# Fifty-six throw-away products on TensorE in four attention-head hand-overs and one output block of a hybrid attention step

## The chip, the cores and the metric

The program runs on one core of one Trainium2 chip, in one launch. The metric is the device time of that launch in microseconds (us), and several executions of the kernel are summarised by their median. The engines are named as in the profile: PE is TensorE, PEld its weight loads, DVE is VectorE, ACT is ScalarE, POOL is GpSimd, SP is the engine that issues most of the transfers.

## The reference

The reference is one layer of a streaming encoder on 512 prompt frames and 64 new frames, 1024 features wide:

```
h   = x + 1/2 * SwiGLU_1(RMSNorm(x))                 # d_ff 2816
u   = RMSNorm(h);  proj = u @ w_in                   # q, k, v of two groups of heads, rotary on q and k
oa  = sliding-window attention with sinks            # group A: 8 query heads, 2 key/value heads, 64 wide
ob  = softmax(q1 k1) v - lam * softmax(q2 k2) v      # group B: 4 heads, 128-wide values, block-causal
ob  = RMSNorm per head and frame (ob) * g_subln * (1 - lam_init)
h   = h + concat(oa, ob) @ w_out
h   = h + 1/2 * SwiGLU_2(RMSNorm(h));  y = RMSNorm(h)
```

It returns y for prompt and new frames, and the new key and value caches.

## The kernel before

All activations lie transposed, features on the partitions and the 576 frames along the free axis, so that one product of a weight block of 128 x 128 covers 288 frames and two of them cover all. For accuracy each weight block and each activation is split into a high part (made by ACT, `w_hi`, L950) and a low part (made by DVE, `w_lo`, L1291), and each product is done three times: high by high, high by low, low by high. These are the products of line L594 (`feature_products`); one step `k` of a block is six of them. The two feed-forward parts take the first 450 us and the last 400 us or so; between them lie projections, attention and the output projection.

The middle part is one list of events, written once by `make_schedule` and walked by every engine, each taking from an event what is its own:

- `k (b, k)`: step k of the projection of q/k tile b, and, for b = 13, of output block 0. They are the filling between the attention steps.
- `S n`: the scores of unit n on PE (L799 for prompt tiles of group B, L803 for the new frames), the row maxima on DVE (L1604 to L1616), the exponentials on ACT (L1184, L1188).
- `N n`: normalising the probabilities on DVE (L1628 to L1639).
- `T r`: transposing them on PE (L828, into PSUM bank `T_BANK`) and copying them to SBUF on ACT (`probs_t`, L1209).
- `O r`: the product with the values on PE (L864, L868), and, after a head's last tile, copying the output out on DVE (`o_b`, L1666, L1668) and squaring it on ACT (L1224).
- `R`: once per B head, the per-head RMSNorm: sum of squares on DVE (L1675), square root on ACT (L1230, with a table load before it), reciprocal and five scalings of `o_b` on DVE (L1682, L1684), which raise `ob_ready`.
- `L`: once per B head, `heads_back`: PE waits for `ob_ready` and transposes the normalised output back (L881 four times, L882 once); ACT writes `mix_hi` (L1238, L1239) and DVE `mix_lo` (L1692, L1695), which raise `mix_ready`.

Each engine works through its own instructions strictly in the order of the list. For heads 0, 1 and 2 the order on all engines around the hand-over is `O` of the next head's first tile, `L`, `T` and `N`, then `S` of the next head's last tile. That last `S` waits on PE for the exponentials of the tile before it, whose PSUM banks it reuses. Of output block 0 (b = 13) the steps 0 to 6 stand between the attention events of heads 2 and 3; its step 7 needs the mix of head 3 and is the last event of all. The end of the list is:

```
T[39](B,3,3)   O[39](B,3,3)   R(head 3)   L(head 3)   k(13,7)
```

After it PE goes through output blocks 1 to 7, eight steps each, in `out_step`. Block 0 waits, at each of its steps, for the part of the mix that this step reads (`if d == 0: pe.wait_ge(mix_ready, ...)`); block 1 waits at its step 0 for the last exponentials and the last mix, since it writes into PSUM banks that attention used. Block d from 2 on waits for the addition of block d - 2 to the residual.

At the start of the program PE does 44 products of a 128 x 128 tile of ones with itself in fp32 (L733, `WARM_UP`), until the first inputs are there. Each product shows as two matmul records in the trace.

Of the kernel before, what the change touches and what calls it, by code (L numbers as in the profile page):

```python
# [25 lines left out]
P = 128  # L26
# [12 lines left out]
B_HEADS = 4  # L39
# [65 lines left out]
def split_base(key):  # L105

    kind = key[0]
    if kind == "qk" and key[1] == len(TILES) - 1:
        return SPLIT_Z
    return (SPLIT_X, SPLIT_Y)[key[-1] % 2]  # L110
# [38 lines left out]


WARM_UP = 44

Y_GP = 2

# [94 lines left out]
def hybrid_step(nc, a, o):  # L249

    stack = ExitStack()
    with stack:
        def sb(name, shape, dt=FP32, where=stack):
            return where.enter_context(nc.sbuf_tensor(name, shape, dt))
# [12 lines left out]
        ones = sb("ones", [P, P])  # L267
# [52 lines left out]
        acc = stack.enter_context(nc.psum_tensor("acc", [P, 8, BANK], FP32))  # L320
# [79 lines left out]
        T_BANK, O_BANK = 6, 7  # L400
# [76 lines left out]
        def mix_tile(n):  # L477
            return UNITS[n][1] + (PAIRS if UNITS[n][0] == "L" else 0)

        def pair(n):  # L480

            return 2 + 2 * (order_at[n] % 2)

        def wait_scores_banks(pe, n):

            if order_at[n] < 2:
                return
            former = bank_order[order_at[n] - 2]
            if UNITS[former][0] == "L":
                pe.wait_ge(mix_ready, mix_count[former])  # L490
            else:
                pe.wait_ge(exp_done, score_at[former] + 1)
# [91 lines left out]
        def _(pe):  # L584
            def block_ready(key):

                pe.wait_ge(split_ready, GROUP[key] + 1)

            def feature_products(bank, base, k_in_block, hi, lo, k, first, last, token_halves=(0, 1)):

                col = base + k_in_block * P
                for n, (w_part, x_part) in enumerate(((w_hi, hi), (w_hi, lo), (w_lo, hi))):
                    for t in token_halves:
                        m = nc.tensor.matmul(acc[:, bank + t, 0:HALF], w_part[:, col:col + P],  # L594
                                             x_part[:, k, t * HALF:(t + 1) * HALF],
                                             start=first and n == 0, stop=last and n == 2)
                return m
# [133 lines left out]

            for _ in range(WARM_UP):
                nc.tensor.matmul(acc[:, NORM_BANK, 0:P], ones[:], ones[:], start=True, stop=True)  # L733
# [3 lines left out]
            for c in range(2):  # L737
                for kc in range(2):
                    key = ("v", 2 * c + kc)
                    block_ready(key)  # L740
                    for tt in range(TOK_TILES):
# [8 lines left out]
                        for k in range(V_K):  # L750
# [4 lines left out]
                            for n, (x_part, w_part) in enumerate(((u_hi, w_hi), (u_hi, w_lo), (u_lo, w_hi))):  # L755
# [3 lines left out]
                                    start=kg == 0 and n == 0, stop=kg == KD - 1 and n == 2)  # L759
# [77 lines left out]
            def values(r):  # L837
# [33 lines left out]
                                         v_new[0:DEC, SEQ_TILES, P * (t + 1):P * (t + 2)], start=False, stop=True)  # L871
                m.then_inc(o_done, 1)

            def heads_back(n):
                h = UNITS[n][1]
                wait_scores_banks(pe, n)

                pe.wait_ge(ob_ready, h + 1)
                bank = pair(n)
                for tt in range(SEQ_TILES):  # L880
                    nc.tensor.transpose(acc[:, bank, tt * P:(tt + 1) * P], o_b[:, h % 2, tt, :], ident[:])  # L881
                nc.tensor.transpose(acc[:, bank + 1, 0:DEC], o_b[0:DEC, h % 2, SEQ_TILES, :],  # L882
                                    ident[0:DEC, 0:DEC]).then_inc(ob_turned, 1)

            def out_step(d, k):

                bank = 2 * (d % 2)
                if k == 0:
                    block_ready(("out", d))
                    if d >= 2:  # L890

                        pe.wait_ge(res_ready, KD + d - 1)
                    elif d == 0:
                        pe.wait_ge(x_out, len(TILES))
                    else:

                        pe.wait_ge(exp_done, len(score_order))
                        pe.wait_ge(mix_ready, mix_count[bank_order[-1]])
                if d == 0:

                    pe.wait_ge(mix_ready, max(c for n, c in mix_count.items() if mix_tile(n) == k))
                m = feature_products(bank, split_base(("out", d)), k, mix_hi, mix_lo, k, k == 0, k == KD - 1)
                if k == KD - 1:
                    m.then_inc(block_used, 1)

            for event in EVENTS:
                if event[0] == "k":
                    _, b, k = event
                    if b == len(TILES):
                        out_step(0, k)  # L910
                        continue
                    if k == 0:
                        block_ready(("qk", b))
                        if b == 0:

                            pe.wait_ge(v_out, TOK_TILES + 2)
                        elif b == 1:

                            pe.wait_ge(v_out, 2 * TOK_TILES)
                        else:  # L920

                            pe.wait_ge(x_out, 1 if b == 2 else b)
                    m = feature_products(tile_bank(b), split_base(("qk", b)), k, u_hi, u_lo, k, k == 0, k == KD - 1)
                    if k == KD - 1:
                        m.then_inc(block_used, 1)
                elif event[0] == "S":
                    scores(event[1])
                elif event[0] == "T":
                    transposes(event[1])
                elif event[0] == "O":  # L930
                    values(event[1])
                elif event[0] == "L":
                    heads_back(event[1])

            for d in range(1, KD):
                for k in range(KD):
                    out_step(d, k)
# [1002 lines left out]
```

## Time and profile before

| | |
|---|---|
| median of 3 runs | 1163.64 us (1162.18 to 1164.63) |
| the profiled execution | 1164.48 us |
| its span, first to last instruction | 1162.7 us |
| PE busy | 1093.1 us, 94% of the span |
| DVE busy | 702.2 us, 60% |
| ACT busy | 477.0 us, 41% |
| POOL busy | 88.7 us, 8% |
| mean granted TensorE clock | 0.968 of full |

The 1.8 us between the span and the execution's own time lie outside the first and the last instruction. In the profile a granted clock of 1.00 is TensorE's full rate of 2.4 GHz and 0.50 is 1.2 GHz. The busy time of a matmul counts from its start to the end of its way through the array, so consecutive matmuls overlap in it; the rate is read from the starts. A profile row gives in brackets the idle time of the engine just before that row and what ended it.

### The profile page before, as it was taken

Reading aid. Unit: us, or ns where it says so; the run is one execution under the profiler, and the core shown is the slowest. Engines: PE = TensorE matmul, PEld = TensorE weight load, DVE = VectorE, ACT = ScalarE, POOL = GpSimd, SP = SyncE. Lnnn points to the kernel's source line nnn. Section 1 sums busy time; section 2 is a strip of 40 time slices with the busy share of each in tenths; the row PEclk is TensorE's granted clock in tenths of the full one; section 3 lists DMA queues with packets and bytes.
Section 4 is the critical chain, followed back from the end, with each engine's and each line's share of the span. In section 5 each row is a group of like instructions: output and inputs, shape, how many; then the busy total and the mean of one; then the engine's idle time right before and its main releaser. Section 6 shows DMA issues by size and latency. Waiting matters only on the chain.

```text
span 1162.7 us, 18955 instructions
## 1 busy us (share of the span) xinstructions
PE 1093.1 (94%) x7874; PEld 1057.8 (91%) x7874; DVE 702.2 (60%) x1046; ACT 477.0 (41%) x803; POOL 88.7 (8%) x84
## 2 busy tenths in 40 slices
PE   9989999999999999778898859999999999999995
PEld 9989999999999999766777639999999999999994
DVE  5887832588863333556677744478883248886324
ACT  6445531256553333223344443334563125555221
POOL 0000000000001111312222102200000000000012
PEclk9999999999999999888999869999999999999997
DMA  5233123222222241300021102223313222222202
GB/s 191 74 109 109 54 97 103 93 81 102 98 76 76 94 140 60 123 19 27 21 73 37 50 1 73 79 84 111 110 50 101 91 105 76 107 96 76 77 26 82
DMA packets 22660, 94.43 MB, mean 81 GB/s; under 512 B 2928, under 2 KB 6000, under 8 KB 18096
## 3 DMA queue, kind: packets, MB, share of 16 engines
q1 hardware_dynamic: 22576, 93.23, 24.0%
q8 instruction: 63, 1.03, 0.4%
q14 instruction: 21, 0.17, 0.0%
HBM read 88.24 MB, written 4.98 MB: 80 GB/s over the span
## 4 chain that ended last, share of the span: by engine, by line
PE 75%; DVE 14%; ACT 6%; issue 4%; POOL 0%; DVEq 0%; ACTq 0%; POOLq 0%
PE acc L594 34%; PE acc L663 33%; PE acc L756 3%; ACT w_hi L950 2%; DVE w_lo L1291 1%; PE acc L733 1%; ACT c_hi L1028 1%; DVE comb L1405 1%; PE acc L851 1%; DVE st L1605 1%; DVE st L1598 1%; ACT probs L1174 1%; ACT probs L1184 1%; DVE probs L1639 1%; DVE res L1740 1%
## 5 line engine op out<-in xcount | busy, mean ns | idle before, releaser
L1291 DVE TENSOR_TENSOR w_lo<-raw,w_hi 128x1024 fp32r<-128x1024 f32 (+3 forms) x145 | 175.5, 1211 | 266.8 <-ACT w_hi L950 266.0
L663 PE MATMUL acc<-c_hi,w_hi 128*128 128x288 f32 x952 | 282.5, 297 | 5.5 <-DVE w_lo L1291 5.5
L663 PE MATMUL acc<-c_lo,w_hi 128*128 128x288 f32 x952 | 283.3, 298 | 0.0
L663 PE MATMUL acc<-c_hi,w_lo 128*128 128x288 f32 x952 | 283.3, 298 | 0.0
L950 ACT ACTIVATE w_hi<-raw 128x1024 fp32r<-128x1024 f32 (+3 forms) x145 | 149.1, 1028 | 190.6 <-PE acc L594 175.3
L594 PE MATMUL acc<-h_hi,w_hi 128*128 128x288 f32 x1024 | 222.7, 297 | 3.9 <-DVE w_lo L1291 3.9
L594 PE MATMUL acc<-h_lo,w_hi 128*128 128x288 f32 x1024 | 221.6, 296 | 0.0
L594 PE MATMUL acc<-h_hi,w_lo 128*128 128x288 f32 x1024 | 221.5, 296 | 0.0
L663 PEld LDWEIGHTS acc<-c_hi,w_hi 128*128 128x128 f32 x952 | 179.9, 189 | 6.0 <-DVE w_lo L1291 6.0
L663 PEld LDWEIGHTS acc<-c_lo,w_hi 128*128 128x128 f32 x952 | 179.8, 189 | 0.0
L663 PEld LDWEIGHTS acc<-c_hi,w_lo 128*128 128x128 f32 x952 | 179.5, 189 | 0.0
L594 PEld LDWEIGHTS acc<-h_hi,w_hi 128*128 128x128 f32 x1024 | 166.0, 188 | 4.8 <-DVE w_lo L1291 4.6
L594 PEld LDWEIGHTS acc<-h_lo,w_hi 128*128 128x128 f32 x1024 | 165.9, 188 | 0.1
L594 PEld LDWEIGHTS acc<-h_hi,w_lo 128*128 128x128 f32 x1024 | 165.9, 188 | 0.0
L1291 DVE TENSOR_TENSOR w_lo<-comb,w_hi 128x1024 fp32r<-128x1024 f32 x68 | 83.3, 1225 | 60.7 <-ACT w_hi L966 60.7
L966 ACT ACTIVATE w_hi<-comb 128x1024 fp32r<-128x1024 f32 x68 | 71.8, 1056 | 68.3 <-PE acc L663 37.6
L1056 ACT ACTIVATE comb<-acc 128x288 f32<-128x288 f32 x136 | 56.1, 412 | 103.2 <-PE acc L663 103.0
L1768 POOL TENSOR_TENSOR ssq<-ssq,sq 128x576 f32<-128x576 f32 x23 | 33.7, 1465 | 848.0 <-issue 720.1
L594 PE MATMUL acc<-u_hi,w_hi 128*128 128x288 f32 x208 | 54.0, 343 | 1.5 <-DVE sq L1579 1.4
L594 PE MATMUL acc<-u_lo,w_hi 128*128 128x288 f32 x208 | 47.4, 312 | 0.0
L594 PE MATMUL acc<-u_hi,w_lo 128*128 128x288 f32 x208 | 47.3, 311 | 0.0
L594 PEld LDWEIGHTS acc<-u_hi,w_hi 128*128 128x128 f32 x208 | 35.8, 205 | 12.3 <-issue 11.8
(198 smaller groups left out, 1327.6 us busy)
## 6 DMA issues: line engine op xcount, KB each, us to landing
raw<-in_w1gu SPq DMA_DIRECT2D x17, 1024.0 KB, 4.8
raw<-in_w2gu SPq DMA_DIRECT2D x17, 1024.0 KB, 4.8
raw<-in_w1d SPq DMA_DIRECT2D x16, 704.0 KB, 4.1
raw<-in_w2d SPq DMA_DIRECT2D x16, 704.0 KB, 4.1
raw<-in_w_qk SPq DMA_DIRECT2D x13, 512.0 KB, 3.6
raw<-in_w1gu SPq DMA_DIRECT2D x10, 512.0 KB, 4.6
raw<-in_w2gu SPq DMA_DIRECT2D x10, 512.0 KB, 3.7
raw<-in_w_out SPq DMA_DIRECT2D x8, 512.0 KB, 3.5
```

Of the source, the lines that this page charges most:

```text
L594: m = nc.tensor.matmul(acc[:, bank + t, 0:HALF], w_part[:, col:col + P], x_part[:, k, t * HALF:(t + 1) * HALF], start=first and n == 0, st ...
L663: m = nc.tensor.matmul(acc[:, banks[side(f)], 0:HALF], w_part[:, col:col + P], x_part[:, k, c, :], start=n in (P1, P5, P2) and k == 0 and ...
L733: nc.tensor.matmul(acc[:, NORM_BANK, 0:P], ones[:], ones[:], start=True, stop=True)
L756: m = nc.tensor.matmul(acc[0:n_tok, V_BANK[tt], 0:V_HALF], x_part[:, kg, tok], w_part[:, split_base(key) + k * V_HALF:split_base(key) + (k ...
L851: m = nc.tensor.matmul(acc[rows, O_BANK, tile * P:(tile + 1) * P], v_new[:, tile - 1 + s, HEAD * part:HEAD * part + HEAD], pt[:, (2 * qi + ...
L950: nc.scalar.activation(cols, src, ACT.Copy).then_inc(hi_ready, 1)
L966: nc.scalar.activation(w_hi[:, first * PART:(first + 2) * PART].rearrange("p (s n) -> p s n", s=2), w_sum[:, 2 * half:2 * half + 2, :], AC ...
L1028: nc.scalar.activation(c_hi[:, j, 1:PARTS, :], b[:, 2:PARTS + 1, :], ACT.Copy).then_inc(chi_ready, 1)
L1056: nc.scalar.activation(to, acc[:, PRODUCTS[n][0][side(f)], 0:HALF], ACT.Copy).then_inc(snapped, 1)
L1174: m = nc.scalar.activation(pr[:, 256 * s:256 * (s + 1)], acc[:, bank + s // 2, 256 * (s % 2):256 * (s % 2 + 1)], ACT.Exp, scale=SCALE, bia ...
L1291: return nc.vector.tensor_tensor(cols, src, hi.bitcast(FP32), ALU.subtract).then_inc(split_ready, 1)
L1768: nc.gpsimd.tensor_tensor(ssq[:], ssq[:], sq[:], ALU.add).then_inc(ssq_added, 1)
```

## The change

`keep_going(n)` is added on PE: n fp32 products of the 128 x 128 tile of ones with itself, written into the first 128 columns of `T_BANK`, which nobody reads. It is called in `heads_back` between the wait for the PSUM banks and the wait for `ob_ready`, with 9 products for heads 0 to 2 and 20 for head 3, and in `out_step` at step 0 of output block 1, between the wait for the block's weights and the waits for the last exponentials and the last mix, with 9 products. In all that is 3 x 9 + 20 + 9 = 56 products. Nothing is removed or moved.

```
+KEEP, KEEP_LAST = 9, 20
...
+            def keep_going(n):
+                for _ in range(n):
+                    nc.tensor.matmul(acc[:, T_BANK, 0:P], ones[:], ones[:], start=True, stop=True)
+
             def heads_back(n):
                 h = UNITS[n][1]
                 wait_scores_banks(pe, n)
+                keep_going(KEEP_LAST if h == B_HEADS - 1 else KEEP)
 
                 pe.wait_ge(ob_ready, h + 1)
...
                     elif d == 0:
                         pe.wait_ge(x_out, len(TILES))
                     else:
 
+                        keep_going(KEEP)
                         pe.wait_ge(exp_done, len(score_order))
                         pe.wait_ge(mix_ready, mix_count[bank_order[-1]])
```

## Rows read from the trace of the kernel before

**Rows 1.** The page: PE's busy tenths and granted clock by slices; the final chain by engine.

```profile
PE   9989999999999999778898859999999999999995
...
PEclk9999999999999999888999869999999999999997
...
PE 75%; DVE 14%; ACT 6%; issue 4%; POOL 0%; DVEq 0%; ACTq 0%; POOLq 0%
```

**Rows 2.** Waits of PE, 480 to 700 us: total, times, longest.

```profile
PE acc L881 <- DVE o_b L1684: 6.7, 4, 4.5
PE acc L799 <- ACT probs L1184: 6.6, 3, 2.3
```

**Rows 3.** Timeline of PE at head 0, and one wait before it.

```profile
603.42 1.16 PE L864 MATMUL acc<-v_new,probs_t 128*128 128x128 f32 x8 [1.13 <-ACT probs_t L1209]
...
616.51 0.63 PE L881 MATMUL acc<-ident,o_b 128*128 128x128 f32 x4 [0.65 <-DVE o_b L1684]
...
617.47 0.44 PE L828 MATMUL acc<-ident,probs 128*128 128x128 f32 x2
620.21 1.22 PE L799 MATMUL acc<-k_b,q_b 64*128 64x512 f32 x4 [2.30 <-ACT probs L1184]
...
631.68 0.60 PE L828 MATMUL acc<-ident,probs 128*128 128x128 f32 x4
```

**Rows 4.** Windows: length, PE busy, granted clock, DMA share, GB/s.

```profile
602.00:604.00 2.00, 0.87 (x9) 1.00 0.00 0
621.20:624.40 3.20, 3.20 (x14) 0.50 0.00 0
648.50:655.10 6.60, 4.98 (x16) 0.50 0.10 37
679.30:682.40 3.10, 1.46 (x11) 1.00 0.00 0
682.60:686.00 3.40, 2.64 (x11) 0.50 0.00 0
694.40:699.60 5.20, 5.20 (x22) 0.50 0.02 3
700.00:747.00 47.00, 47.00 (x355) 1.00 0.26 84
```

**Rows 5.** Timelines of PE at heads 2 and 3.

```profile
671.36 0.63 PE L881 MATMUL acc<-ident,o_b 128*128 128x128 f32 x4 [0.77 <-DVE o_b L1684]
...
675.05 2.08 PE L799 MATMUL acc<-k_b,q_b 64*128 64x512 f32 x4 [2.05 <-ACT probs L1184]
...
684.48 2.07 PE L864 MATMUL acc<-v_new,probs_t 128*128 128x128 f32 x8 [0.69 <-ACT probs_t L1209]
...
691.03 1.09 PE L881 MATMUL acc<-ident,o_b 128*128 128x128 f32 x4 [4.48 <-DVE o_b L1684]
692.05 0.37 PE L882 MATMUL acc<-ident,o_b 64*128 64x64 f32 x1
694.37 0.85 PE L594 MATMUL acc<-mix_hi,w_hi 128*128 128x288 f32 x2 [1.96 <-DVE mix_lo L1695]
```

**Rows 6.** The warm-up: its timeline row, then windows as in rows 4.

```profile
1.08 12.77 PE L733 MATMUL acc<-ones 128*128 128x128 f32 x88 [1.08 <-DVE eps L1347]
...
3.00:5.00 2.00, 2.00 (x11) 1.00 0.93 339
7.50:9.50 2.00, 2.00 (x20) 1.00 1.05 429
```

**Rows 7.** Timelines of ACT and DVE after heads 0 and 1.

```profile
619.96 0.69 ACT L1238 ACTIVATE mix_hi<-acc,lam 128x512 fp32r<-128x512 f32 x1
...
631.89 0.01 DVE L1577 LOAD_MASK_SELECT ssq<-acc  x1 [0.81 <-PE acc L594]
...
661.89 0.16 DVE L1628 RECIPROCAL st<-st 128x1 f32<-128x1 f32 x1 [0.90 <-ACT probs L1188]
```

**Rows 8.** The final chain after head 2 and at head 3.

```profile
682.68 1.13 PE acc L828 x4
...
689.81 1.08 DVE o_b L1684 x5
...
694.37 48.20 PE acc L594 x342
```

More of the change, by code:

```diff
@@ L151 @@
 WARM_UP = 44
+KEEP, KEEP_LAST = 9, 20
 Y_GP = 2
@@ L872, in values, with keep_going @@
                 m.then_inc(o_done, 1)
+            def keep_going(n):
+                for _ in range(n):
+                    nc.tensor.matmul(acc[:, T_BANK, 0:P], ones[:], ones[:], start=True, stop=True)
             def heads_back(n):
@@ L876, in heads_back @@
                 wait_scores_banks(pe, n)
+                keep_going(KEEP_LAST if h == B_HEADS - 1 else KEEP)
                 pe.wait_ge(ob_ready, h + 1)
@@ L895, in out_step @@
                     else:
+                        keep_going(KEEP)
                         pe.wait_ge(exp_done, len(score_order))
```

## The prediction

> **What bounds the kernel now.** I read the page first: PE is near full for most of the run and carries 75% of the chain that ended last, but in the middle, slices 16 to 23, its busy share and its granted clock dip together [rows 1]. The change lives there. The list of PE's waits says what it stood for: the normalised output of the four B heads (`ob_ready`), 6.7 us in four waits with the longest of 4.5, and the exponentials before a head's last scores, 6.6 us in three waits of up to 2.3 [rows 2]. The timeline of one hand-over shows their order: at head 0 PE waits 0.65 us at L881, transposes, waits 2.30 us at L799, and then runs without a gap to 631.68 [rows 3]. Head 1 repeats it. The windows give the second price of such waits: right after the pair of waits at head 0 the clock is at 0.50 (1.2 GHz) from about 621.2 to 624.4, after head 1 from 648.5 to 655.1, and at head 3 from 682.6 to 699.6 but for nothing in between [rows 4]. The work runs at half rate there: from 694.4 to 699.6 some 21 matmuls start in 5.2 us, 0.24 us each, against 353 in 47.0 us at full clock, 0.133 us each (the counts less one or two already under way) [rows 4].
>
> So a throw-away product can do three things: nothing (the wait was longer and the clock stays as it was), cost its own time (where PE would have worked), or buy clock for the real work behind it.
>
> **What a product costs.** The warm-up is the same operation on the same operands. Its 88 records start over 12.5 us [rows 6]. At full clock 20 records are seen in 2.0 us, some two of them already under way, so 0.111 us for one; early on, at half rate, 11 in 2.0 us, less one or two, 0.2 to 0.223; I take twice 0.111, 0.223 [rows 6]. (The granted clock is printed as 1.00 there, since the trace has no record of it before its first change; the rate of the records tells the level.) A product is two records: 0.22 us at full clock, 0.45 at half. Nine are 2.0 us (4.0 at half), twenty 4.45 us (8.9 at half).
>
> **Heads 0 to 2, nine products each.** The products start where PE came free, some 0.7 us before its L881 row [rows 3, 5], take 2.0 us, and so push L881 back by about 1.3 us. What is queued behind them on PE is the transposes L881 and L882 and the next tile's L828, 1.3 us of work, then the scores at L799. Who waits for L881: ACT's `mix_hi`, which at head 0 starts only at 619.96, behind the exponentials; the transposes end at about 617.4 now and would end at 618.7. L828's copy on ACT comes behind `mix_hi`. So both are covered by ACT's exponentials, with about 1.2 us left, and the scores themselves wait for the exponentials until 620.21 as before. Direct cost: nothing. If that cover were gone it would be 1.3 us a head.
>
> What they may buy is the clock. The 2.30 us wait shrinks to about 1.0, and the first wait vanishes. The trace has a wait of 1.13 us at 603.42 behind which the clock stayed at 1.00 [rows 3, 4]; behind 0.65 and 2.30 it fell. The rest is nearer to the first, so I take it that the clock holds after heads 0 and 1 more often than not. What is that worth? At head 0, 3.4 us at half rate hold up work by about 1.5 to 1.9 us, all of it ahead of L828 at 631.68. But DVE, which takes the projection tile from PE at 631.89, had then stood idle for only 0.81 us [rows 7]: before that it was busy with the next tile's maxima and could not have taken it sooner. So of 1.9 us only 0.8 arrives: -0.8 us. After head 1 the same stretch ends in DVE waiting for ACT at 661.89, not for PE [rows 7]; ACT's exponentials there follow DVE's maxima, which follow the split of the next weights, none of it waiting for PE. There I take 0. Head 2: behind it the final chain stays on DVE and ACT until the transposes at 682.68 [rows 8], so whatever the clock does from 672 to 679 changes nothing; and then PE is too short of work to keep the clock: 0 again. Sum for the three heads: -0.8, with bounds of 0 (clock falls anyway) and -0.8 for head 0, and some -0.4 more for head 1 at best.
>
> One rule of the Trainium skill speaks against the holding. "TensorE: Matmul & The Clock Gate", section "A second HAM failure mode: psum-queue depth-cycling", says that short idles between groups of matmuls, often repeated, can make the clock swing too. The trace agrees in that waits of 0.65 and 2.30 us with work between were enough, though the 1.13 us wait was not. By that rule the -0.8 would be 0; it is one of the rivals below.
>
> **Head 3, twenty products.** Here ACT and DVE are on the path from the values at 684.48 to `ob_ready` at about 690.9, and PE is free from about 686.5 [rows 5, 8]. The clock is at 0.50 when the products begin: it fell at 682.6, and from 686 to 691 nothing here can have raised it but the products themselves [rows 4]. All at half rate they end at 686.5 + 8.9 = 695.4; all at full rate at 691.0. How soon does a run of them raise the clock? The warm-up shows the rate doubled between the windows 3 to 5 and 7.5 to 9.5, having started at 1.08 [rows 6]; head 0's stretch shows a return 3 to 4 us after dense work began at 620.21 [rows 3, 4]. With the same here, the values at 684.48 already being dense, I put the return at about 689.4. Until then 2.9 / 0.223 = 13 records, and the other 27 take 27 x 0.111 = 3.0 us: end at 692.4. That is 1.4 us later than L881's 691.03. In return L881 and L882 run at full clock: at head 0 they take 0.96 us from the first to the next instruction, here 1.39 to the end, so about 0.5 us is won. Net +0.9 us on the path, since ACT's `mix_hi` and DVE's `mix_lo` follow at once and PE waits for both [rows 5]. Bounds: the return at 688 gives +0.1 (end at 691.7), the return 5.6 us after 686.5 as late as in the warm-up gives an end of 693.8 and +2.2, and no return at all +4.4.
>
> **Output block 1, nine products.** The name of the change speaks of a wait there. There is none: PE resumes at 694.37 with step 7 of block 0, the 1.96 us wait before it is for DVE's `mix_lo` of head 3 [rows 5], and from there the final chain is one piece of PE work of 342 products in 48.2 us [rows 8]. The two waits behind the call were already met by step 7 of block 0, which needs the same mix. So the nine products lie fully on the path: 18 x 0.111 = +2.0 us. At half clock they take 4.0, but then they also use up half-rate time in which real work would have stood, so the net is again 2.0. Nothing later gives it back, since block after block follows PE, and the sums and the second feed-forward part follow those. Bounds: 1.9 to 2.4.
>
> **The clock when PE resumes.** Before, PE ran 5.2 us at half rate after 694.4 [rows 4], which cost 5.2 x (1 - 0.133 / 0.24) = 2.3 us. Afterwards the products leave PE at full clock when head 3's transposes are done; then comes the untouched wait of 1.96 us. It is nearer to the 2.05 to 2.30 us waits behind which the clock fell [rows 3, 5] than to 1.13. So I take it to fall, but from full clock, with the half-rate stretch as long as head 0's 3.4 us rather than 5.2: 3.4 x 0.446 = 1.5 us lost, that is -0.8. Bounds: 0 (as long as before), -2.3 (never falls).
>
> **Sum.** -0.8 + 0.9 + 2.0 - 0.8 = +1.3 us, against the profiled execution's 1164.48. The median of the runs shown is 0.84 lower, 1163.64, so the forecast is 1164.9 us. A measurement of this kernel can tell about 0.2%, 2.3 us, from no change.
>
> **The rivals.**
> - The clock holds over the last wait too. For it: PE is dense before and behind it. Against: the length. Then -2.3 in place of -0.8: -0.2, 1163.4 us. Still no change that can be told.
> - The skill's short idles: nothing is held after head 0 either. +2.1, 1165.7 us.
> - Faster: the clock holds through head 2's end to the values of head 3, so L828 and L864 run at full rate: 0.5 + 0.9 us, from 1.13 to 0.6 and from 2.07 to 1.16 [rows 3, 5, 8]. The twenty then begin at 685.1 at full clock, end with `ob_ready`, and cost nothing; the gain of 0.5 at L881 stays, and the last wait holds. -0.8 - 1.4 - 0.5 + 2.0 - 2.3 = -3.0, 1160.6 us. Against it: from 679.3 to 682.4 PE starts only 11 matmuls at full clock and then falls [rows 4], and no product is put there.
> - Slower: the twenty overrun. It decides from a return of the clock later than about 691.4, which puts their end at 693.4: then +1.9 at head 3, +2.0 at the output block, -0.8 at resuming and 0 or -0.8 at head 0, +2.3 to +3.1. With the warm-up's 5.6 us it is +2.2 + 2.0 + 0 + 0 = +4.2, 1167.8 us; with no return at all +6.4, 1170.0 us.
> - The change does nothing, every product hidden: 1163.6. Against it stands the missing wait at the output block.
>
> **How the numbers follow.** Forecast 0.48, clock held over the last wait 0.19, nothing held 0.10, all these within 0.2% of before; faster 0.07; slower 0.16, of which most near +3. A few hundredths of the forecast's own spread pass each bound, since three runs of the same kernel already lie 2.4 us apart: faster 0.08, same 0.73, slower 0.19. The range leaves out the faster case and half of the slower one: 1161.9 to 1167.2.
>
> **What would show it.** L881 at head 0 near 617.8 and L799 still near 620.2, with 1.00 in the windows from 621 to 624; the last 0.8 us earlier at DVE's L1577. At head 3, forty records of the new line from 686.5 (less what head 0 won) to about 692.4, with 0.50 turning to 1.00 near 689.4, and L881 directly behind them with no idle. Eighteen records between step 7 of block 0 and block 1, with no idle next to them. The forecast is wrong if L881 of head 3 still waits for `ob_ready` (then the twenty are hidden and the sum falls by 0.9 or more), if the clock at resuming stays at 1.00 or stays at 0.50 for 5 us, or if PE had idle time ahead of block 1.

## The result, and the profile after

The changed kernel takes 1165.1 us (median of 19 executions, 1163.5 to 1169.89) against 1163.62 us before (19 executions, 1161.8 to 1164.82). The ratio is 1.0020, 95% interval 1.0011 to 1.0028, that is +2.3 us, from +1.3 to +3.3. The forecast was +1.3 us, 1164.9 us. So the total came out near the forecast, but, as the experiments show, partly for another reason.

The profiled execution of the changed kernel is the slowest of the 19 (1169.89 us, span 1168.1 us). 2.7 us of its distance to the profile of before lie ahead of the first product added for the heads: the tile of scores that DVE starts to reduce at 573.68 us before is started at 576.37 us here. From there on the two can be compared stage by stage.

The timeline of PE in the changed kernel, with the added products on L880, the transposes of the heads on L890 and L891, the scores on L801, values on L866 (rows 3 and 5 of before answer to it):

```profile
618.37 2.17 PE L880 MATMUL acc<-ones 128*128 128x128 f32 x18
620.38 0.60 PE L890 MATMUL acc<-ident,o_b 128*128 128x128 f32 x4
620.91 0.28 PE L891 MATMUL acc<-ident,o_b 64*128 64x64 f32 x1
621.12 0.44 PE L830 MATMUL acc<-ident,probs 128*128 128x128 f32 x2
622.87 1.13 PE L801 MATMUL acc<-k_b,q_b 64*128 64x512 f32 x4 [1.32 <-ACT probs L1194]
...
662.03 0.66 PE L830 MATMUL acc<-ident,probs 128*128 128x128 f32 x4 [1.39 <-DVE probs L1649]
662.62 0.49 PE L801 MATMUL acc<-k_b,q_b 64*128 64x128 f32 x4
664.24 1.59 PE L866 MATMUL acc<-v_new,probs_t 128*128 128x128 f32 x8 [1.13 <-ACT probs_t L1219]
665.62 2.21 PE L835 MATMUL acc<-diag,probs 128*128 128x64 f32 x10
...
674.78 0.59 PE L866 MATMUL acc<-v_new,probs_t 128*128 128x128 f32 x2 [2.10 <-ACT probs_t L1219]
675.17 3.74 PE L880 MATMUL acc<-ones 128*128 128x128 f32 x18
678.75 0.60 PE L890 MATMUL acc<-ident,o_b 128*128 128x128 f32 x4
...
690.67 5.31 PE L880 MATMUL acc<-ones 128*128 128x128 f32 x40
695.83 0.60 PE L890 MATMUL acc<-ident,o_b 128*128 128x128 f32 x4
...
698.59 0.59 PE L596 MATMUL acc<-mix_hi,w_hi 128*128 128x288 f32 x2 [1.96 <-DVE mix_lo L1705]
...
699.94 3.32 PE L880 MATMUL acc<-ones 128*128 128x128 f32 x18
703.02 0.51 PE L596 MATMUL acc<-mix_hi,w_hi 128*128 128x288 f32 x2
```

At head 0 the products fill the first wait and push back the transposes, and the scores still wait, now 1.32 us instead of 2.30 [rows 3]. At head 3 the forty records run straight into the transposes with no idle between. In output block 1 the eighteen records stand between real products with no idle on either side. New against before are the 1.39 us wait at 662.03 and what follows it. Before, PE had no wait at the same transposes (L828) and a shorter one at the values behind them:

```profile
660.83 0.60 PE L828 MATMUL acc<-ident,probs 128*128 128x128 f32 x4
...
662.39 1.16 PE L864 MATMUL acc<-v_new,probs_t 128*128 128x128 f32 x8 [0.55 <-ACT probs_t L1209]
```

The windows of the changed kernel's profile (length, PE busy, granted clock, DMA share, GB/s) say what the clock did:

```profile
623.00:650.00 27.00, 25.88 (x187) 1.00 0.07 20
665.00:671.50 6.50, 6.50 (x29) 0.50 0.00 0
675.10:678.30 3.20, 3.20 (x17) 0.50 0.01 3
688.90:692.00 3.10, 3.10 (x15) 0.50 0.00 0
699.00:702.20 3.20, 3.20 (x16) 0.50 0.00 0
703.50:750.00 46.50, 46.50 (x351) 1.00 0.25 80
```

The half-rate stretches after heads 0 and 1 [rows 4] are gone. In their place there is one from 665 to 671.5, where PE was at full clock before. And the chain that ended last shows that this one counts:

```profile
664.24 1.59 PE acc L866 x8
665.83 2.01 PE acc L835 x10
667.84 1.16 PE acc L801 x4
668.99 1.90 PE acc L870 x8
670.89 0.63 PE acc L872 x2
...
674.78 0.59 PE acc L866 x2
675.37 3.54 PE acc L880 x18
678.91 0.44 PE acc L890 x4
...
690.88 5.11 PE acc L880 x40
```

Head 2's nine products, mostly at half rate, are themselves on the chain for 3.54 us, and head 3's twenty for 5.11 us.

To compare kernels in spite of what happened to the clock earlier in each execution, I split each profile at the starts of five DVE instructions that all the kernels have: the reduction of the new frames' scores of head 0 (L1607, 573.68 us before), the taking of projection tile 11 behind head 0 (631.89, the L1577 of [rows 7]), the copy of head 3's output (L1668, 686.59), head 3's first `mix_lo` (L1692, 693.38), and the split of weights that follows output block 1 (L1291, 705.35). The stages, in us, are differences of these starts; "last" runs to the end of the span, and "mix to block 1" holds PE's resuming and output block 1:

| profile of | to tile 11 (head 0) | to head 3's output (heads 1, 2) | to mix_lo (head 3) | mix to block 1 | last |
|---|---|---|---|---|---|
| before | 58.21 | 54.70 | 6.79 | 11.97 | 457.35 |
| changed | 57.32 | 57.23 | 6.67 | 13.26 | 457.25 |
| e1 heads only | 57.34 | 57.28 | 6.64 | 11.16 | 460.24 |
| e2 block only | 58.21 | 54.72 | 6.79 | 14.03 | 458.75 |
| e3 head 3 only | 59.55 | 54.31 | 7.92 | 9.66 | 458.85 |
| e4 heads 0 to 2 only | 57.35 | 57.35 | 6.79 | 11.17 | 460.07 |
| e5 feed-forward waits only | 58.20 | 54.75 | 6.79 | 11.91 | 457.34 |
| e6 nearly all waits | 57.34 | 53.62 | 6.17 | 9.65 | 456.91 |
| e7 heads and mix wait | 57.34 | 54.82 | 7.19 | 9.65 | 458.81 |
| e8 block twice | 59.52 | 54.35 | 6.79 | 16.55 | 460.29 |
| e9 heads 0 to 2, later waits | 57.34 | 56.24 | 6.78 | 11.63 | 457.30 |
| e10 heads 0 to 2, feed-forward | 57.34 | 57.38 | 6.79 | 11.20 | 457.29 |
| e11 placed by wait | 57.35 | 53.68 | 6.18 | 9.66 | 457.40 |
| e12 twelve at head 3, mix wait | 58.19 | 54.81 | 6.18 | 9.65 | 460.32 |

Each profile is one execution; the medians and ratios below are over 5 to 12 executions of each kernel, with 27 to 35 of before beside them.

### The profile page after: what moved, and what is told of

It reads as the page before. It is cut to its first block, busy times and chain, and to the rows that moved or that the text cites. A ratio compares the mean times of both kernels' runs of the same rounds, so it can differ in the third digit from the quotient of the medians.

```text
span 1168.1 us, 19175 instructions
## 1 busy us (share of the span) xinstructions
PE 1105.5 (95%) x7986; PEld 1072.1 (92%) x7986; DVE 702.0 (60%) x1046; ACT 476.7 (41%) x803; POOL 88.6 (8%) x84
## 4 chain that ended last, share of the span: by engine, by line
PE 75%; DVE 15%; ACT 6%; issue 3%; POOL 0%; DVEq 0%; ACTq 0%; POOLq 0%
PE acc L596 34%; PE acc L665 33%; PE acc L758 3%; ACT w_hi L960 2%; DVE w_lo L1301 2%; PE acc L735 1%; PE acc L880 1%; PE acc L853 1%; DVE st L1615 1%; ACT c_hi L1038 1%; DVE comb L1415 1%; ACT probs L1194 1%; DVE probs L1649 1%; DVE st L1608 1%; ACT probs L1184 1%
```

## The experiments

**The change taken apart.** Four kernels were measured together: the four heads without the block, the block without the heads, head 3 alone, and heads 0 to 2 alone.

```
e1: KEEP_AT, KEEP_OUT = (9, 9, 9, 20), 0     e2: (0, 0, 0, 0), 9
e3: (0, 0, 0, 20), 0                         e4: (9, 9, 9, 0), 0
+                keep_going(KEEP_AT[h])      # heads_back
+                        keep_going(KEEP_OUT)   # out_step, block 1
```

> The change without the nine products of output block 1 (heads 9, 9, 9, 20 stay). Theory 1, the nine lie bare on PE's path: 2.0 us below the changed kernel, about 1163.1 us and the ratio to before near 1.000 (0.9985 to 1.0005). Theory 2, the nine are hidden or pay for themselves in clock, and the loss comes from the heads: no faster than the changed kernel, 1165.1 us, ratio 1.0013 or more.

Measured: 1161.07 us (1159.31 to 1168.47), ratio 0.9994, interval 0.9978 to 1.0010. By the medians it is 4.0 us below the changed kernel, which was timed on another occasion; by the ratios, each against runs of before of its own occasion, it is 0.26%, 3.0 us. That is at least the 2.0 us of theory 1; theory 2 does not fit. The 12 executions are far apart: eight between 1159.3 and 1162.4 us with a mean granted clock of 0.977 to 0.981, four between 1165.8 and 1168.5 us with 0.973.

> Only the nine products of output block 1, none in the heads. Theory 1: before plus 2.0 us, 1165.6 us, ratio 1.0017. Theory 2: as before, ratio 1.000. In the profile 18 records of the new line with no idle on either side by theory 1; idle shortened by as much by theory 2.

Measured: 1164.76 us (1162.78 to 1168.58), ratio 1.0019, interval 1.0006 to 1.0033. That is theory 1, and its profile shows it without detour:

```profile
691.92 0.85 PE L596 MATMUL acc<-mix_hi,w_hi 128*128 128x288 f32 x2 [1.96 <-DVE mix_lo L1705]
...
693.52 3.84 PE L880 MATMUL acc<-ones 128*128 128x128 f32 x18
697.12 0.51 PE L596 MATMUL acc<-mix_hi,w_hi 128*128 128x288 f32 x2
```

No idle on either side; and the stage from the mix to block 1 is 14.03 us against 11.97, +2.06 us. The records ran mostly at half rate, 3.6 us from the first to the next real product, and the net is 2.06 all the same. PE is at half rate for 5.1 us after it resumes here (691.92 to 697.0) and for 5.2 us before (694.37 to 699.6), so the real work that the products displaced ran at full rate behind them.

> Only the twenty products of head 3. Forecast's step: they begin at half clock, overrun ob_ready by about 1.4 us and win 0.5 us in the transposes and 0.8 us or more after PE resumes: between +0.1 and -0.9 us, ratio 0.9992 to 1.0001. If the twenty end by ob_ready: -1.3 us or better, ratio 0.9985 to 0.999. If their overrun outweighs the clock: +1 us or more, ratio 1.001.

Measured: 1161.94 us (1159.88 to 1164.61), ratio 0.9993, interval 0.9984 to 1.0002, inside what the forecast's step gave. In the profile the products cost and won more than forecast: they pushed head 3's `mix_lo` from 6.79 to 7.92 us (+1.13), and afterwards the clock held while PE waited for the mix, so that the next stage took 9.66 us instead of 11.97 (-2.31):

```profile
686.02 6.56 PE L880 MATMUL acc<-ones 128*128 128x128 f32 x40
692.42 0.60 PE L890 MATMUL acc<-ident,o_b 128*128 128x128 f32 x4
692.95 0.27 PE L891 MATMUL acc<-ident,o_b 64*128 64x64 f32 x1
695.19 0.54 PE L596 MATMUL acc<-mix_hi,w_hi 128*128 128x288 f32 x2 [1.97 <-DVE mix_lo L1705]
```

The clock held over the wait of 1.97 us with no product in it, as in the forecast's rival of the last wait.

> Only the nine products of each of heads 0, 1 and 2. Forecast's step: -0.8 us from head 0 and nothing from the others, ratio 0.9993. The rival, read from the profile of the changed kernel, is that the clock that they hold up is only taken away later, between the values of heads 1 to 3, where PE's work is on the path: a half-rate stretch near 665 us in its profile costs 2.4 us, so that the sum is between +0.5 and +1.5 us, ratio 1.0005 to 1.0013, in the executions that have it, and -0.8 in the others: more spread than before.

Measured: 1166.85 us (1163.31 to 1168.18), ratio 1.0027, interval 1.0017 to 1.0038. This is the surprise: the three heads' products, forecast at -0.8 us, lose 3.1 us. Its profile is the best pair to that of before, since until 566 us the clock changes at the same places within 0.3 us. By the table it wins 0.86 us at head 0, loses 2.65 between heads 1 and 3, wins 0.8 when PE resumes, and loses 2.72 in the last stage, where the two kernels have not one instruction that differs. The windows at the three places:

```profile
662.00:668.70 6.70, 6.70 (x30) 0.50 0.00 0
...
768.00:771.00 3.00, 3.00 (x14) 0.50 0.49 168
815.60:818.90 3.30, 2.87 (x12) 0.50 0.00 0
```

The chain of e4 carries the same two things as that of the changed kernel: values and transposes at half rate from 661.5 us, and head 2's products:

```profile
661.49 1.69 PE acc L866 x8
663.17 2.01 PE acc L835 x10
...
672.90 3.35 PE acc L880 x18
```

The last stage shows one wait twice. This is the timeline row of before, then that of e4:

```profile
766.08 0.54 PE L594 MATMUL acc<-h_hi,w_hi 128*128 128x288 f32 x2 [1.76 <-DVE w_lo L1291]
```

```profile
766.94 0.53 PE L596 MATMUL acc<-h_hi,w_hi 128*128 128x288 f32 x2 [1.76 <-DVE w_lo L1301]
```

The wait is 1.76 us in both, PE was full ahead of it in both, and in before the clock stayed at 1.00, also over the 2.54 us wait at 811 to 814 us:

```profile
764.00:767.00 3.00, 1.24 (x10) 1.00 0.01 1
811.00:814.50 3.50, 0.96 (x8) 1.00 0.00 0
814.50:818.00 3.50, 3.50 (x28) 1.00 0.32 42
```

In e4 it fell behind both. So the length of a wait does not settle whether it costs clock. The program here is the same in both kernels and the wait comes 0.86 us later in e4, so I take it that the moment at which it comes counts too; no run tests this by itself. The changed kernel's own profile happens to have none of these falls in its last stage (457.25 us).

**Is it the waits of the feed-forward parts?** The next four kernels were measured together. The products of the first two are written into the PSUM bank that the following work overwrites, or into `T_BANK` where nothing in it is still to be read, and the wait for the data comes behind them. For this some waits of PE were put into another order, and every kernel but e8 from here on has that order, also at the waits where it has no products; no kernel measures the new order by itself. In their profiles the stages without new products are within 0.11 us of those in the old order (57.34 us in e7 and in e1; 58.19 and 54.81 in e12, 58.21 and 54.70 before).

```
e5: FILL = {gate/up (0,2,up): 8, pair (0,5): 11, gate/up (1,1,up): 7, pair (1,5): 9}
+                keep_in(FILL.get(("gu", ffn, f, part), 0), acc[:, bank, 0:P])
                 block_ready(key)
```

> No products in the heads or in output block 1; instead 8, 11, 7 and 9 products in the four waits of the feed-forward parts (near 47, 81, 764 and 811 us). Theory A, raised by the runs so far: what these kernels differ in is largely whether the clock falls behind those waits, which hangs on where they come and not on their length alone. Then no half-rate stretch is left near 48, 85, 768 and 816 us, the median is 1.5 us below before (1161.2 us, ratio 0.9985 to 0.999) and the slow end of the spread (1167 us) is gone. Theory B, the spread has another origin: the spread stays and the ratio is 1.000 or above, by the products' own time.

Measured: 1163.15 us (1160.07 to 1164.15), ratio 0.9988, interval 0.9978 to 0.9998. The slowest of the 12 took 1164.15 us. Of the 27 of before on this occasion one took 1166.64 us and the others at most 1165.05, which is too little to say that a slow end is gone. The profile of e5 has no half-rate stretch in either feed-forward part up to the last wait of the run, and the last stage is 457.34 us. Theory A held in the profile and in the ratio; the median fell by 0.6 us and not by 1.5, and what it says of the spread stays open.

> Products in nearly every wait of PE over 1 us, none in output block 1: those of the feed-forward parts, 9, 9, 9 and 18 in the heads, 7 ahead of the wait for head 3's mix, and 79 in nine waits of the attention part. Theory A: nearly all half-rate stretches go, the mean clock is above 0.985, and where PE is on the path behind them it shows: 6 to 12 us below before, ratio 0.990 to 0.995. Theory B: the products cost about what they win, ratio 0.998 to 1.002.

There were in fact 93 products in ten waits of the attention part. Measured: 1160.91 us (1159.84 to 1164.66), ratio 0.9978, interval 0.9967 to 0.9989. The mean clock rose to 0.990 and the gain was 2.6 us, not 6 to 12. One reason stands in its timeline, at the longest wait of PE:

```profile
506.54 7.37 PE L596 MATMUL acc<-ones 128*128 128x128 f32 x44 [4.53 <-ACT probs_t L1241]
```

Ahead of the products PE waited 4.53 us for a copy by ACT, so the clock was already low when they began, and only some 1.4 us were left of the 5.9 us wait that they were to fill. They took 7.37 us: DVE's last `mix_lo` ahead of this place was done at 507.8 us, and the values behind it started at 513.83. Such products ahead of 575 us cost 3.2 us in all (its new frames' scores of head 0 are reduced from 575.51 us, those of e5 from 572.31); behind them every stage of e6 is the shortest or nearly so, 5.3 us below before in all.

```
e7: the change, with block 1's nine products out and
+                    if k == KD - 1:   # step 7 of block 0, ahead of the wait for head 3's mix
+                        keep_in(7, acc[:, T_BANK, 0:P])
```

> The change with the nine products of output block 1 taken out and 7 put where PE does wait, ahead of the mix of head 3 (step 7 of block 0). By the forecast's arithmetic the clock then holds when PE resumes: 1.5 us below the kernel with the heads' products alone, 3.5 us below the changed kernel: median near 1160 to 1161 us, ratio 0.9975 to 0.9985, and no half-rate stretch near 697 to 700 us. If the clock falls there all the same: as with the heads' products alone, 0.9994.

Measured: 1162.36 us (1159.54 to 1164.32), ratio 0.9989, interval 0.9978 to 1.0001. In the profile PE resumes at full clock and the stage is 9.65 us, against 11.16 with the heads alone and 13.26 in the changed kernel. That step is as forecast; the median came out 1.4 us above the top of what was expected, and its 12 executions lie in two groups, four up to 1160.4 us and eight from 1162.1 us. Here the clock fell at 647.7 us instead of 662, behind the 1.34 us that are left of head 1's wait for the exponentials, and PE then came later to the work of 657 to 664 us. That costs nothing: 54.82 us from head 0 to head 3's output, as before. Head 2's nine products ran at full rate and are not on the chain. In the changed kernel the same wait at head 1 is 1.33 us long and the clock held over it.

> Only output block 1, with 18 products in place of 9, none in the heads. If a product there costs its own 0.222 us and nothing else: +4.0 us, ratio 1.0034, twice that of nine. By theory A the total is +4.0 us give or take the stretches behind the waits near 765 and 812 us, which come later against the clock's changes: the lower group of its runs at +4 - 1.5 or +4, an upper one 2 to 4 us above.

Measured: 1168.88 us (1166.09 to 1171.96), ratio 1.0047, interval 1.0029 to 1.0066. The stage of block 1 grew by 4.58 us in the profile, 2.2 times the 2.06 of nine; 18 x 0.222 = 4.0 us of it are the products' own time at full clock. Of the rest, 0.5 us, the profile shows a longer stretch at half rate: 6.1 us after PE resumed, against 5.2 before. The last stage was 460.29 us.

**What becomes of the three heads' products.** The last four were again measured together.

```
e9:  KEEP_AT (9, 9, 9, 0), e5's FILL, and {O[33]: 5, T[34]: 5, O[34]: 4}
e10: KEEP_AT (9, 9, 9, 0), e5's FILL
e11: KEEP_AT (9, 9, 9, 18), e9's FILL, {O[24]: 4, O[36]: 8, O[38]: 10, O[39]: 3}, mix: 7
e12: KEEP_AT (0, 0, 0, 12), mix: 7
```

> The nine products of heads 0, 1 and 2 (none at head 3, none in block 1), with 14 more in the three waits of the stretch from 657 to 662 us behind head 1's hand-over, and 35 in the waits of the feed-forward parts. Theory C: the three heads' products lose because the clock that they held is then taken away behind those later waits, where PE's values and transposes are on the path, and head 2's products, run at half rate, come on the path too. Then with those waits filled the half-rate stretch near 662 to 669 us is gone in most executions, the stretch from head 0's tile hand-over to head 3's values is back from 57.3 to 54.7 us or less, and the median is 2 us or more below before, ratio 0.998. Rival: the three heads' products cost time of their own: the stretch stays at 57.3 us.

> As the run above but without the 14 products of 657 to 662 us: the nine of heads 0 to 2 and the 35 of the feed-forward parts. Theory A: the last 457 us (after output block 1) come back from 460.0 us to 457.3 us, since the clock no longer falls behind the waits near 765 and 812 us; the loss of 2.6 us between heads 1 and 3 stays: ratio near 1.0005, against 1.0027 with the heads' products alone. Rival, the loss of the heads' products lies wholly in the attention part: ratio 1.002 or more.

Measured: e10 1163.40 us (1161.5 to 1165.7), ratio 1.0002, interval 0.9993 to 1.0011; e9 1163.13 us (1161.8 to 1164.62), ratio 1.0002, interval 0.9994 to 1.0011. In e10 the last stage is back at 457.29 us and 0.25% of e4's 0.27% is gone, although the stretch between heads 1 and 3 is as long as in e4 (57.38 us). Not all of the 0.25% was e4's loss, though: the same 35 products won 0.12% without any in the heads (e5), and they also fill the two waits ahead of 100 us. The remaining 0.13%, about half of e4's 0.27%, is what the three heads' products cost at the feed-forward waits, which they don't touch; each of these differences is uncertain by some 0.1%. Against e5, e10 is still 0.14% slower. Theory A's number (1.0005) held.

Theory C of e9 held only in part. The 14 products kept the clock over the waits at 657 to 662 us, but then it fell at 667 us, in the next wait, and head 2's nine products ran at half rate and on the chain again:

```profile
667.94 0.77 PE acc L886 x2
668.71 3.84 PE acc L900 x18
```

The stage is 56.24 us, between 54.70 and 57.38, and the median gains nothing over e10.

> Only head 3: 12 products instead of 20 there, and 7 ahead of its mix. With 20, L881 came 0.5 to 1.1 us late and directly behind the products in two profiles. With 12 they end well before ob_ready even at half rate (686.5 + 5.3 = 691.8 at worst): the stretch from head 3's values copied out to its mix_lo is 6.3 to 6.8 us, against 6.8 before and 7.9 with 20 alone, and PE resumes at full clock, 6.3 us for block 1's stretch against 7.9. Together -2.3 us, ratio 0.998. If 12 are too few to hold or raise the clock: 4.09 and 7.9 us as before, ratio 1.000.

Measured: 1163.08 us (1158.13 to 1165.16), ratio 0.9992, interval 0.9979 to 1.0005. In the profile both stages came out as expected, 6.18 and 9.65 us, together 2.9 us below before; the last stage gave 3.0 us back, with half rate behind both feed-forward waits:

```profile
765.20:768.20 3.00, 3.00 (x14) 0.50 0.44 152
813.00:816.00 3.00, 3.00 (x13) 0.50 0.01 3
```

The ratio lies between the two that were expected (0.998 and 1.000). The best execution took 1158.13 us; it was not profiled, so that it had none of these falls is a guess.

> What the runs point to: 9, 9, 9 and 18 products in the heads, 7 ahead of head 3's mix, none in block 1, 25 in the waits on copied probabilities of the last tiles, the 14 of 657 to 662 us and the 35 of the feed-forward parts; none in the waits before 600 us, where the kernel with products in nearly all waits lost 3.6 us. From its stretches: -1.9 us before 92 us, -0.9 at head 0, -1.0 to head 3, -0.6 in head 3, -2.3 when PE resumes, -0.4 after: 1157 us, ratio 0.9945, at least 0.3% below the changed and the old kernel.

Measured: 1158.20 us (1156.09 to 1159.18, 5 executions), ratio 0.9956, interval 0.9944 to 0.9968: 5.1 us faster than before by the ratio, close to what was expected (0.9945), and the fastest of all. Every stage behind 574 us is at or near its shortest. From 615 to 675 us and from 679 to 1146 us its clock is at 1.00, with one fall between:

```profile
615.00:675.00 60.00, 54.43 (x394) 1.00 0.12 34
675.40:678.60 3.20, 3.00 (x13) 0.50 0.00 0
679.00:1146.00 467.00, 460.24 (x3446) 1.00 0.24 79
```

## Why the prediction was right, and where it was right by luck

**The price of a product** held: 18 records of head 0 take 2.0 us from their start at 618.37 to the transposes at 620.38, 0.112 us each; 0.111 was forecast.

**Head 0, -0.8 us**: the stage measured 58.21 before and 57.32 to 57.35 in every profile that has the products there, -0.87. The forecast had limited the gain by DVE's 0.81 us of idle time at its L1577 rather than by what PE lost at half rate, and for this profile that was the right limit. It is not the limit in every execution: the stage took 59.55 us in e3 and 59.52 in e8, which have no products there either. In these two the clock stayed low for 6.8 us behind the same waits and not for 3.4; against them the products win 2.2 us.

**Heads 1 and 2, 0 us**: this step failed, and in place of nothing there were two losses. First, the products' own time was held to be covered, worked out at full rate, and at head 2 the clock was to change nothing, "whatever the clock does from 672 to 679". At full rate, 2.0 us, they are covered (e7); mostly at half rate the nine take 3.5 us and are on the chain. Second, the forecast asked where the work behind a kept clock would gain and not where PE would then stand idle next. PE reached 657 to 664 us early, waited 1.39 and 1.13 us for DVE and ACT, and the clock fell there, ahead of values and transposes that are on the chain. Together +2.5 us in the profile (54.70 to 57.23), in e4 +2.65. By e9, whose nine are slow but whose values ahead of them are not, some 1.5 us of this belong to the first loss; that is an estimate, since e9 has 14 more products. Where the clock fell elsewhere, as in e7, the loss was 0.1 us. And the stage had something to give: with the next waits filled too, e6 and e11 took 53.62 and 53.68 us.

**Head 3, +0.9 us**: the mechanism is right, the size too large for the changed kernel. The products ran directly into the transposes, and the stage took 6.67 us instead of 6.79, because the clock rose 1.5 us after they began and not 2.9. The transposes started 0.6 us after `o_b` was scaled, where the forecast had them 1.4 us late. In e7 it rose after 2.5 us and the stage was 7.19, +0.40; in e3 after 4.1 us, 7.92, +1.13. So the term hangs on when the clock rises, as the forecast said. Twelve products do it in 6.18 us (e12).

**Output block 1, +2.0 us**: +2.10 (13.26 against 11.16 in e1), +2.06 (e2 against before). PE had no wait there, as the forecast read from the order of the list.

**Resuming, -0.8 us**: e1 against before is 11.16 to 11.97, -0.81, and in the changed kernel the clock fell from full behind the wait, for 3.4 us, as forecast. But that the size came out is luck. e4 and e10, with no product at head 3 and the clock already low through the wait, have 11.17 and 11.20 us: PE resumed in e4 at 696.06 and was back at full clock at 699.5, 3.4 us too. So these profiles do not show that head 3's products earned the 0.8 us. With 7 products ahead of this wait the clock held (e7, e12: 9.65), and in e3 it held without them (9.66), so that they are needed is not shown either.

**What the sum left out**: the waits near 765 and 812 us. One fall behind them costs about 1.45 us (457.35 to 458.8), two 2.9 (460.2). The profile of before has neither; the other kernels shift by up to a few microseconds what comes at them, and their profiles have one, both or none. This, with heads 1 and 2, is a loss the forecast did not have. Against it stands only the smaller cost at head 3. That the total nevertheless stayed near +1.3 is no merit of the forecast: the median rose by 1.5 us, the ratio says +2.3, and the changed kernel's profile has no late fall while e4's has two. The stage table adds up for the profiled pair: -0.89 + 2.53 - 0.12 + 1.29 - 0.10 = +2.7 us, and another 2.7 us of that profile lie ahead of the change.

Of the rivals, nothing held after head 0 did not happen, though short waits did cost clock elsewhere. The Trainium skill, "TensorE: Matmul & The Clock Gate", section "A second HAM failure mode: psum-queue depth-cycling", says that short idles between groups of matmuls, when they come often enough, make the clock swing. The runs agree in so far as waits of 1.40 and 1.13 us with work between them did it at 662 us in e4. They do not agree for head 0 of the changed kernel, where a single 1.32 us wait was left and the clock held. The other rival, the clock held over the last wait, came true in e3 and not in the changed kernel.

What stays open: what sets the moments at which a wait costs clock. Kernels with the same instructions from 700 us on take the late falls in one profile and not in another, so the order of the instructions there does not settle it. And why e4's executions take the late falls so often is read from the profile of one of them and from e10, not from each of the twelve.

## What to carry to other kernels

A throw-away product is free only in a wait that the engine really has, at the slower of its two rates: read the wait from the timeline, not from the code, and count the products at half clock (nine were 2.0 us at full and 3.5 us mostly at half; at 0.445 us each, the forecast's figure for half rate, a wait of 2 us takes an estimated four). A clock kept up early is not a gain by itself: follow the engine to its next waits, since that is where it fell in these profiles; filling some waits and not the next ones lost 3.1 us, filling them in a row up to the dense work, and the feed-forward waits with them, won 5.1 us. And when an edit shifts the end of a half-rate stretch, code far behind it can change by more than the edit: compare stages between fixed instructions, and fill the late waits in both kernels before judging an early one.

## What the runs showed of the hardware that was not expected

- The same wait of 1.76 us ahead of the same matmuls left the granted clock at 1.00 in one profile (766 us, before) and took it to 0.50 in another (767 us, e4); a 2.54 us wait at 813 us left it at 1.00 in before. A fall costs about 1.45 us there.
- A kernel's executions spread by 3 us before (1161.8 to 1164.82; on another occasion one of 35 took 1167.22) and by 6 to 9 us with some of the edits (1163.5 to 1169.89, and 1159.31 to 1168.47 for e1), with the mean granted clock going along with the time: 0.977 to 0.981 below 1163 us, 0.973 above 1165 us in e1.
- More clock is not more speed by itself: e6 ran at a mean granted clock of 0.990 and took 1160.91 us, e11 at 0.980 in its profile and took 1158.20 us, though e6 was 2.4 us behind it when head 0's scores were reduced (575.51 against 573.13 us), after products that ran past their wait.
